# Output projection of the token mixer as split products, in a transformer kernel on one core

## What is computed

```python
        attn_out = sliding_window_attention_with_sinks(q, k, v, sinks[l])
        pool_out = causal_pool_mixer(u, pool_w[l], pool_scale[l])
        mix = jnp.concatenate([attn_out, pool_out], axis=-1) @ w_out[l]
        x = x + gate_m * rms_norm(mix, g_post_mix[l])

        h = rms_norm(x, g_pre_ffn[l]) * (1.0 + scale_f) + shift_f
        f = (jax.nn.silu(h @ w_gate[l]) * (h @ w_up[l])) @ w_down[l]
```

## Time and profile before

| | us |
|---|---|
| median of 3 runs | 2691.64 |
| lowest and highest run | 2689.56, 2692.16 |
| the profiled execution | 2685.79 |
| its span | 2684.0 |

### The profile page before, as it was taken

The page is one execution under the profiler, slowest core; times in us unless marked ns, Lnnn a source line. Parts: engine busy times, 40 slices in busy tenths (PEclk is TensorE's granted clock), DMA queues, the critical chain, the costliest instruction groups (busy, mean ns, idle before and its releaser), DMA issues.

```text
span 2684.0 us, 27025 instructions
## 1 busy us (share of the span) xinstructions
PE 2417.9 (90%) x10972; PEld 1692.1 (63%) x10972; DVE 1015.1 (38%) x1647; ACT 819.6 (31%) x1214; POOL 165.2 (6%) x229
## 2 busy tenths in 40 slices
PE   5988999999888999998899999999999699998782
PEld 4744888788744888787777777776888433333230
DVE  3433222236333222235888886342335400000003
ACT  3233222225233222234666663233222111111102
POOL 1000000001000000001000000000001211111112
PEclk8988999999988999999999999999999699999996
DMA  8391332323352222224222222222324599999994
GB/s 307 110 360 63 94 94 79 106 82 107 133 189 63 94 94 79 73 86 116 55 63 55 71 95 84 70 63 63 94 95 169 219 397 409 393 415 415 416 391 193
DMA packets 212042, 439.93 MB, mean 164 GB/s; under 512 B 10028, under 2 KB 151516, under 8 KB 190928
## 3 DMA queue, kind: packets, MB, share of 16 engines
q1 hardware_dynamic: 202544, 417.42, 42.6%
q0 software_dynamic: 9376, 20.80, 2.2%
HBM read 433.45 MB, written 15.99 MB: 167 GB/s over the span
## 4 chain that ended last, share of the span: by engine, by line
PE 56%; DVE 6%; DMA 5%; ACT 4%; SPq 2%; issue 2%; POOL 1%; POOLq 0%; DVEq 0%; ACTq 0%
PE psum L912 37%; PE psum L1454 6%; DMA arena<-in_w 4%; PE psum L1477 3%; PE psum L1097 2%; SPq L645 2%; PE psum L1233 1%; PE psum L1261 1%; PE psum L1325 1%; PE psum L1253 1%; SPq L651 1%; PE psum L1316 1%; DVE arena L2429 0%; DMA arena<-x_rows,arena 0%; PE psum L1391 0%
## 5 line engine op out<-in xcount | busy, mean ns | idle before, releaser
L912 PE MATMUL psum<-split,split 128*128 128x512 f32 (+2 forms) x6432 | 1503.4, 395 | 34.1 <-DVE split L2098 10.4
L912 PEld LDWEIGHTS psum<-split,split 128*128 128x128 f32 x6432 | 1217.4, 190 | 299.6 <-issue 32.2
L2098 DVE TENSOR_TENSOR split<-arena,split 128x1024 fp32r<-128x1024 f32 x132 | 161.5, 1225 | 492.4 <-ACT split L1584 492.1
L1454 PE MATMUL psum<-arena 128*64 128x512 f32 x1184 | 274.5, 617 | 27.9 <-DMA arena<-in_w 27.2
L1584 ACT ACTIVATE split<-arena 128x1024 fp32r<-128x1024 f32 x132 | 139.4, 1058 | 521.4 <-PE psum L912 521.4
L1454 PEld LDWEIGHTS psum<-arena 128*64 128x64 f32 x1184 | 98.1, 142 | 199.1 <-issue 164.7
L2798 DVE TENSOR_TENSOR arena<-arena,psum 128x256 f32<-128x256 f32 x37 | 15.6, 420 | 450.3 <-ACT arena L1963 450.3
L1477 PE MATMUL psum<-arena 128*64 128x512 f32 x592 | 135.2, 597 | 21.0 <-issue 19.7
L1097 PE MATMUL psum<-arena 128*128 128x512 f32 x256 | 111.2, 592 | 0.0
L1477 PEld LDWEIGHTS psum<-arena 128*64 128x64 f32 x592 | 46.7, 136 | 85.6 <-issue 85.6
L1963 ACT ACTIVATE arena<-psum 128x256 f32<-128x256 f32 x37 | 14.2, 384 | 274.5 <-PE psum L1454 274.5
(11 more groups left out here) (355 smaller groups left out, 2103.3 us busy)
## 6 DMA issues: line engine op xcount, KB each, us to landing
arena<-in_w SPq DMA_DIRECT2D x93, 2048.0 KB, 21.0
arena<-in_ada_w SPq DMA_DIRECT2D x16, 2048.0 KB, 10.7
arena<-in_w_in SPq DMA_DIRECT2D x56, 512.0 KB, 5.4
arena<-in_w_gate SPq DMA_DIRECT2D x22, 1024.0 KB, 5.4
arena<-in_w_up SPq DMA_DIRECT2D x22, 1024.0 KB, 8.0
arena<-in_w_down SPq DMA_DIRECT2D x12, 1536.0 KB, 6.3
arena<-in_ada_w SPq DMA_DIRECT2D x16, 1024.0 KB, 7.2
arena<-in_w_in SPq DMA_DIRECT2D x16, 1024.0 KB, 6.5
```

The source lines that it names most:

```text
L912: m = nc.tensor.matmul(out, stationary(a), moving(b), start=start and n == 0, stop=stop and n == 2)
L1454: m = nc.tensor.matmul(psum[CAP * half:CAP * half + CAP, 2 + par], xsT[:, par, k % 4, CAP * (k // 4):CAP * (k // 4) + CAP], w13_half(pair, ...
L2098: v.tensor_tensor(mlp_pieces[mlp_at(p)][:, 1], mlp_raw(l, p)[1], mlp_pieces[mlp_at(p)][:, 0].bitcast(F32), ALU.subtract).then_inc(sem("mlp ...
```

## The change

- The mixer's output projection uses `product`: 48 split matmuls a tile instead of 16 plain ones. The loop over the chunks k is now outside the loop over the column halves c, so the transposes stand after k = 3, which is halfway through a tile.
- The mixed features are split as they are evicted: ScalarE's evictions write the high parts, and VectorE subtracts these from the same PSUM bank for the low parts (`pooled_lo`, `attn_lo`). TensorE waits for the low parts before it reuses the banks. VectorE normalises block 3 ahead of `attn_lo` of block 2.
- w_out is loaded by halves of its rows. Each piece (one chunk k, 1024 columns) is copied by ScalarE (`out_hi`) into one of the next two ring slots, units named "high" that load nothing, and subtracted in place by VectorE (`out_lo`). Pieces 0 to 3 follow ScalarE's and VectorE's work of attention block 2, pieces 4 to 7 that of block 3.
- The first two gate/up units now follow the w_out and "high" units in the ring, so their loads are issued when the output projection is done with these slots.
- The semaphores of c and the identity are merged, and those of the input weights' highs and lows are shared with w_out.

```diff
-        units += [("out", l, j) for j in range(OUT_UNITS)]
+        units += [("out", l, j) for j in range(OUT_UNITS)] + [("high", l, j) for j in range(OUT_UNITS)]
...
-    if kind == "out":
+    if kind in ("out", "high"):
         return "out_mm", T * (l + 1)
...
+        mixed_lo = [view_r(at, (4, S)) for at in (region + S, mixer_top)]
...
+        def mixed_part(a, k):
+
+            return (hT_hi, mixed_lo)[a][k // 4][:, k % 4]
+
+        def mixed_w(l, k):
+            at, high = (UNIT_AT[kind, l, k // 4] % RING * SLOT + k % 4 * PIECE for kind in ("out", "high"))
+            return view(arena, at, (PIECE,)), view_r(high, (PIECE,)), view_r(at, (PIECE,))
...
+                if kind == "high":
+                    return
...
+                    sp.dma_start(slot.rearrange("p (k n) -> p k n", k=4), w[:, 4 * j:4 * j + 4, :]).then_inc(done, 16)
...
-                        pe.wait_ge(sem("poolT_ready"), 4 * l + (g - 1))
+                        pe.wait_ge(sem("mixed_lo"), 2 * T * l + (g - 1))
...
-                        pe.wait_ge(sem("attnT_ready"), 4 * l + n)
+                        pe.wait_ge(sem("mixed_lo"), 2 * T * l + T + n)
...
-                pe.wait_ge(sem("attnT_ready"), 4 * l + 4)
-                w_halves = [need("out", l, c).rearrange("p (k n) -> p k n", k=KD) for c in range(OUT_UNITS)]
                 for i in range(T):
+                    if i == 0:
+                        pe.wait_ge(sem("poolT_ready"), 4 * l + 4)
+                        pe.wait_ge(sem("attnT_ready"), 4 * l + 4)
+                        pe.wait_ge(sem("mixed_lo"), 2 * T * (l + 1))
...
-                    for c in range(OUT_UNITS):
-                        for k in range(KD):
-                            m = nc.tensor.matmul(bank(2 * (i % 2) + c), mixT[:, k, i * P:(i + 1) * P], w_halves[c][:, k],
-                                                 start=k == 0, stop=k == KD - 1)
-                            if c == 1 and k == KD // 2 - 1 and i:
...
+                    for k in range(KD):
+                        if i == 0:
+                            pe.wait_ge(sem("layer_lo"), LAYER_PIECES * l + IN_PIECES + k + 1)
+                        _, high, low = mixed_w(l, k)
+                        for c in range(2):
+                            for m in product(bank(2 * (i % 2) + c), lambda h: mixed_part(h, k)[:, i * P:(i + 1) * P],
+                                             lambda h: (high, low)[h][:, 512 * c:512 * c + 512], k == 0, k == KD - 1):
+                                pass
+                        if k == KD // 2 - 1 and i:
+                            if i >= 3:
+                                features_ready(2 * l + 1, i - 3)
+                            elif i == 1:
+                                pe.wait_ge(sem("gate_taken"), l + 1)
+                            to_features(2 * l + 1, i - 1, 4 + 2 * ((i - 1) % 2))
...
-            act.wait_ge(sem("c_in"), 16)
+            act.wait_ge(sem("first_in"), 32)
...
+                def out_hi(k):
+                    raw, high, _ = mixed_w(l, k)
+                    n, h = UNIT_AT["out", l, k // 4], UNIT_AT["high", l, k // 4]
+                    act.wait_ge(ready[n % RING], loaded_at[n])
+                    name, count = unit_freed(h - RING)
+                    act.wait_ge(sem(name), count)
+                    nc.scalar.activation(high, raw, ACT.Copy).then_inc(sem("layer_hi"), 1)
...
                     take_probsT(n)
+                    if n >= 2:
+                        for k in range(4 * (n - 2), 4 * (n - 2) + 4):
+                            out_hi(k)
...
+                def attn_lo(n):
+                    cols = slice(n * P, (n + 1) * P)
+                    dve.wait_ge(sem("attnT_ready"), 4 * l + n + 1)
+                    v.tensor_tensor(mixed_lo[0][:, :, cols], bank(0).rearrange("p (k t) -> p k t", k=4),
+                                    hT_hi[0][:, :, cols].bitcast(F32), ALU.subtract).then_inc(sem("mixed_lo"), 1)
+
+                def out_lo(k):
+                    raw, high, low = mixed_w(l, k)
+                    dve.wait_ge(sem("layer_hi"), LAYER_PIECES * l + IN_PIECES + k + 1)
+                    v.tensor_tensor(low, raw, high.bitcast(F32), ALU.subtract).then_inc(sem("layer_lo"), 1)
...
-                    normalise(n)
+                    if n < T - 1:
+                        normalise(n)
+                    if n == T - 2:
+                        normalise(n + 1)
+                    attn_lo(n)
+                    if n >= 2:
+                        for k in range(4 * (n - 2), 4 * (n - 2) + 4):
+                            out_lo(k)
```

More of the change, by code:

```diff
@@ L132 @@
 IN_PIECES = 4 * IN_UNITS
+LAYER_PIECES = IN_PIECES + KD
 WEIGHED, SQUARED, NORMED = (1, 2, 4, 7), (3, 6, 9, 11), (5, 8, 10, 12)
@@ L523, in build @@
             twice = kind == "gu" or kind == "mod" and MOD_GROUPS[l][0] == GATES
-            arrivals[n % RING] += 32 if twice else 16
+            arrivals[n % RING] += 0 if kind == "high" else 32 if twice else 16
             loaded_at.append(arrivals[n % RING])
@@ L540, in _ @@
         def _(sp):
-            sp.dma_start(ccol, A["c"].rearrange("b (p k) -> p (b k)", p=P)).then_inc(sem("c_in"), 16)
-            sp.dma_start(ident, K["ident"]).then_inc(sem("ident_in"), 16)
+            sp.dma_start(ccol, A["c"].rearrange("b (p k) -> p (b k)", p=P)).then_inc(sem("first_in"), 16)
+            sp.dma_start(ident, K["ident"]).then_inc(sem("first_in"), 16)
             def load(n):
                 kind, l, j = UNITS[n]
+                if kind == "high":
+                    return
                 if n >= RING:
@@ L559, in load @@
                         sp.dma_start(dst, w[:, :, c:c + MOD_W]).then_inc(done, 16)
-                elif kind in ("in", "out"):
-                    name, at, width = ("w_in", IN_AT[j], IN_WIDTHS[j]) if kind == "in" else ("w_out", 512 * j, 512)
-                    w = A[name][l].rearrange("(k p) n -> p k n", p=P)
+                elif kind == "out":
+                    w = A["w_out"][l].rearrange("(k p) n -> p k n", p=P)
+                    sp.dma_start(slot.rearrange("p (k n) -> p k n", k=4), w[:, 4 * j:4 * j + 4, :]).then_inc(done, 16)
+                elif kind == "in":
+                    at, width = IN_AT[j], IN_WIDTHS[j]
+                    w = A["w_in"][l].rearrange("(k p) n -> p k n", p=P)
                     sp.dma_start(slot[:, 0:KD * width].rearrange("p (k n) -> p k n", k=KD),
@@ L956, in _ @@
             modulation(0, 0)
-            pe.wait_ge(sem("ident_in"), 16)
+            pe.wait_ge(sem("first_in"), 32)
             for i in range(T - 1):
@@ L970, in project @@
                         if i == 0 and k % 2 == 0:
[L971 removed]
+                            pe.wait_ge(sem("layer_lo"), LAYER_PIECES * l + 4 * c + k // 2 + 1)
                         _, hi, lo = in_piece(l, c, k // 2)
@@ L1029, in _ @@
                 pe.wait_ge(sem("qkT_ready"), 6 * l + 6)
-                pe.wait_ge(sem("poolT_ready"), 4 * l + 4)
+                pe.wait_ge(sem("mixed_lo"), 2 * T * l + T)
                 def scores(n):
@@ L1566, in in_hi @@
                     act.wait_ge(sem("down_mm"), T * l)
-                nc.scalar.activation(hi, raw, ACT.Copy).then_inc(sem("in_hi"), 1)
+                nc.scalar.activation(hi, raw, ACT.Copy).then_inc(sem("layer_hi"), 1)
             def take_modulation(g):
@@ L1603, in _ @@
                     act.wait_ge(sem("poolw_mm"), 4 * l + (g + 1))
-                    nc.scalar.activation(mixT[:, 4 + g], bank(6 + g % 2), ACT.Copy, scale=pscale[:, l, g:g + 1]
+                    nc.scalar.activation(mixed_part(0, 4 + g), bank(6 + g % 2), ACT.Copy, scale=pscale[:, l, g:g + 1]
                                          ).then_inc(sem("poolT_ready"), 1)
@@ L2091, in in_lo @@
                 raw, hi, lo = in_piece(l, c, q)
-                dve.wait_ge(sem("in_hi"), IN_PIECES * l + 4 * c + q + 1)
-                v.tensor_tensor(lo, raw, hi.bitcast(F32), ALU.subtract).then_inc(sem("in_lo"), 1)
+                dve.wait_ge(sem("layer_hi"), LAYER_PIECES * l + 4 * c + q + 1)
+                v.tensor_tensor(lo, raw, hi.bitcast(F32), ALU.subtract).then_inc(sem("layer_lo"), 1)
             def mlp_lo(l, p):
@@ L2176, in _, with pooled_lo @@
                         m.then_inc(sem("rope_done"), 1) if i == T - 1 and b else C.link(m)
+                def pooled_lo(g):
+                    dve.wait_ge(sem("poolT_ready"), 4 * l + g + 1)
+                    v.scalar_tensor_tensor(out=mixed_part(1, 4 + g), in0=bank(6 + g % 2), scalar=pscale[:, l, g:g + 1],
+                                           in1=mixed_part(0, 4 + g).bitcast(F32), op0=ALU.mult, op1=ALU.subtract
+                                           ).then_inc(sem("mixed_lo"), 1)
+                def attn_lo(n):
[7 more added lines that the diff above has]
+                    v.tensor_tensor(low, raw, high.bitcast(F32), ALU.subtract).then_inc(sem("layer_lo"), 1)
                 for g in range(POOL_G):
@@ L2179, in _ @@
```

(3 more changed lines are left out.)

8 lines of the change are left out of this document (2 added, 6 removed).

## The result

| | before | changed kernel |
|---|---|---|
| median, us | 2691.09 (7 runs, 2689.56 to 2692.16) | 2701.27 (7 runs, 2698.84 to 2701.67) |
| ratio | | 1.0038, 95% interval 1.0028 to 1.0048 |
| the profiled execution, us | 2685.79 | 2698.84 |
| its span, us | 2684.0 | 2697.0 |

The change costs 10 us by the medians. The page has TensorE's busy time 5 us lower and its share of the span at 89% instead of 90%: the work went down and the waiting went up.

The account below looks back on a forecast made before the run. TensorE, busy for 90% of the span, was taken to bound the projection. Products after their wait -7.0, projection clock +4.8, ScalarE's queue +7.1 and +3.4 gave +8.3 us on 2691.64: 2700, range 2692 to 2709.

Parts of the forecast that it names:

- Price of the split product: Output projection: 0.232 us per split product, three against 0.858 for a plain one; 2.6 us less per tile.
- The wait in the middle of a tile: Projection tiles 1 to 3: TensorE waits 2.15 us for VectorE's scaled row before the transposes, leaving 7.0 us saved in all.
- The clock behind the gaps: Projection: half of the six new gaps lower TensorE's clock, 1.6 us each, 4.8 us lost, between 0 and 9.6.
- ScalarE's queue in layer 0: Attention block 3: weight copies waiting for w_out delay probsT evictions 5.0 us; low clock adds 2.1; 7.1 us lost.
- ScalarE's queue in layer 1: Attention block 3: copies waiting for the highs' slot delay probsT evictions 2.4 us; even chance of 2.1 for clock; 3.4 lost.
- The sum: Whole kernel: -7.0 + 4.8 + 7.1 + 3.4 = +8.3 us, giving 2700.
- What was said to be hidden: Copies and subtractions of pieces 4 to 7, and later gate/up loads with 4 us to spare, cost no time.
- (a): Projection and attention: the clock never falls in the new gaps; sum +0.4 us, 2692; chance 0.14.
- (b): Projection and attention: every gap cools, and the gates behind the attention too; +16 us, 2708; chance 0.12.
- (c): Projection tiles 1 to 3: the wait isn't binding, products give their whole 21 us; 2681; chance 0.04.
- (d): Attention: weights land early, only the copies' own 2 to 3 us per layer remain; about +1 us, 2692.5; chance 0.08.
- (e): Projection: a plain product costs 0.43 us, the split one 0.27 more; 128 add 34 us; 2736; chance 0.01.

Follow-up runs that it names:

- The kernel with both parts moved: Changed kernel with all eight weight copies and subtractions behind attention block 3 and transposes behind k = 5 instead of k = 3: 2668.94 us, ratio 0.9921.
- The other tests of it: Transposes behind k = 4, all weight copies behind block 3: 2673.35 us; kernel before, plain products, transposes after the first column half: 2696.59 us.
- the kernel with late transposes: Changed kernel with the transposes of tile i-1 behind k = 5 instead of k = 3: 2680.36 us, ratio 0.9961.

## Why the prediction was right, point by point

It said 2700; the median is 2701.27, and the kernel is 10.2 us slower where 8.3 was forecast. By its own steps, in the profiled executions:

- **Price of the split product: right.** 48 in 11.34 us, less the 0.17 of drain, is 0.233 us each; 0.232 was taken from the down projection. The halving of the FP32 peak in the Trainium skill, "Perfetto Trace Analysis", section Engine Utilization, gives an estimated 0.43 us for one matmul of this shape; taken for a whole plain product, as the prediction's rival took it, it would have made the change's products a loss. The trace has 0.429 us for each of the two records of a plain product (13.73 / 32), so the page's figure agrees with a record, and a plain product costs two. The prediction's "some 16 us per layer" for that rival is 17 (64 x 0.27), as its own 34 for both layers says. The kernel with both parts moved shows a gain of 19.9 us from the products, against 21 forecast.
- **The wait in the middle of a tile: right.** 2.15 us was forecast; 2.21, 2.09 and 2.18 stand in layer 0. The other tests of it gave 0.71 to 0.82 for a forecast of 0.76, and 0.77 to 0.89 for 0.85.
- **The clock behind the gaps: right in kind, a little high.** Half of the six gaps at 1.6 us, 4.8, was taken. Two of six fell in this execution, at 12.90 - 11.34 = 1.6 each, 3.1. Over the four profiles that leave these gaps as they are it was 10 of 24, a little under the half that was taken. Both projections together gave -2.7 us, for -2.2 forecast, and that closeness is in part luck: without the clock they gave -5.9 instead of -7.0, and the clock cost 3.1 instead of 4.8.
- **ScalarE's queue in layer 0: right.** 5.0 us late and 2.1 for the clock were forecast. From the issue of w_out to the first probsT eviction it took 17.8 us instead of 12.6, 5.2 late; from there to the end of the attention matmuls 7.0 instead of 4.5, 2.5 for the clock. The 0.4 us hoped for from longer rows did not come.
- **ScalarE's queue in layer 1: the wait right, the clock put at half.** 3.4 us was forecast: 2.4 for the wait and an even chance of 2.1 for the clock. TensorE in order of time, before and changed:

```profile
779.24 1.14 PE L1055 MATMUL psum<-arena 128*128 128x128 f32 x8 [0.25 <-ACT arena L1623]
```

```profile
791.31 1.97 PE L1072 MATMUL psum<-arena 128*128 128x128 f32 x8 [2.31 <-ACT arena L1646]
```

The wait grew by 2.1 us, and the order behind it took 7.0 us instead of 4.5, 2.5 for the clock: 4.6 in all. The clock fell in all four profiles in which this wait of 2.3 us was left alone; why it falls more surely there than in the projection was not tested. From the first scores to the first product it took 70.8 us instead of 65.7, 5.1 more. The rest of that is 0.8 us ahead of block 3, less 0.3 that the first product comes earlier behind the attention. In block 1 the product with the values took 3.73 us instead of 2.02, the low clock again, ahead of the weight copies.
- **The sum.** Read to the first product of each layer, the profiles give 7.6 us for ScalarE's queue in layer 0 and 4.3 in layer 1. With -2.7 for the projections that is 9.2 us, against 8.3. The other 3.8 of the 13.0 us between the two spans lie ahead of the waits and between the layers, where unchanged code scatters by as much. The medians' 10.2 is nearer to the terms than the spans are.
- **What was said to be hidden was hidden.** No idle time stands ahead of the first product in either layer, even with all eight copies behind block 3, and the first gate/up product waits 5.20 us behind the last transposes, as before, for VectorE's split and not for its load. What lay between the start and the issue of w_out, 2.6 us, was not forecast: some 1.6 of it is the clock in the pooling (12.4 us from the pooling's gap to the first scores, 10.7 before), which fell in the other layer before.
- **The rivals.** (a) and (b) were the ends of the clock's share, and the profile lies between them. (c), the wait not binding, is what the kernel with late transposes makes true, and it took 2680.36 us, where (c) counted 2681. (d) fell, since the load took 13.5 us and not 3 us less than 13.2. (e) fell with the price of the products.

## What to carry to other kernels

When a product gets faster, recount what its length covered: a step placed "halfway" or "three quarters through" is a distance in time, and here one number (k = 5 for k = 3) was worth 17 us in the rows and 20.8 in the median. Work put ahead of a queue's next eviction costs its wait too, all of it, if another engine takes turns with that queue; put it behind the last such eviction, and check that the first user needs its pieces one by one. The change is a gain of 21 us, 0.8%, in the right two places and a loss of 10 in the wrong ones.

## What the runs showed of the hardware that was not expected

- Gaps of 1.9 to 2.3 us between bursts of matmuls bring TensorE's clock to the 1.2 GHz level in some cases and not in others: 10 of 24 in this projection (four profiles), and 15 of 20 behind the gap of 2.3 us in the pooling (ten profiles, two layers). Gaps of 0.7 to 0.9 us in the projection did not in any of twelve. A fall cost 1.6 us of matmul time in the projection and 2.5 us in an attention block.
- Filling such gaps with work that nobody needs kept the clock at 1.00. It took 3.3 us out of the two projections, and 2.5 us out of each attention block; the medians fell by 3.5 and 2.2 us, which is not clear of noise.
- The runs of the kernel before spread from 2685.6 to 2692.5 us (22 runs). Falls of the clock like these may be a part of that; it was not tested.
